# Forming one weight sum of a Strassen-like product by accumulating DMA transfers instead of VectorE adds

## Chip, cores and metric

The kernel runs on one core of a Trainium2 chip. The metric is the device time of one execution in microseconds. TensorE multiplies, VectorE and ScalarE work on tiles, GpSimd is nearly unused here, and SyncE (SP) and ScalarE issue the DMA transfers of the kernel before.

## The reference

One decoder layer on 512 tokens of width 2048: RMSNorm, one wide input projection, three branches (differential attention, dilated attention, gated short convolution), three sigmoid gates, an output projection and a final norm. All in float32. What matters here is the part of the projection that yields branch C's four inputs and the three gates:

```python
proj = jnp.einsum('bsd,df->bsf', h, w_in[l])
...
gates = jax.nn.sigmoid(parts[9 + 3 * n_g] + gate_b[l]).reshape(bsz, seq, N_BRANCH, D_MODEL)
u = jnp.pad(cc * cx, ((0, 0), (C_CONV - 1, 0), (0, 0)))
conv = sum(conv_w[l][j] * u[:, j:j + seq] for j in range(C_CONV))
yc = cb * conv * jax.nn.silu(cz)
merged = (gates[:, :, 0] * jnp.einsum('bsw,wd->bsd', ya, w_branch_a[l]) + ...)
```

## The kernel before, in words

TensorE works in float32r, a reduced form of float32, and recovers the precision by splitting each operand into a high and a low part; every product is three matmuls (lines 519 to 521). ScalarE makes the high half of a weight unit (128 x 1024) into one of three slots w_hi (line 841), VectorE the low half w_lo (line 1227), and TensorE uses the slot for 12 matmuls. A slot can be filled again when TensorE is through with it, so ScalarE and VectorE run up to three units ahead.

The first half of the kernel (to about 1440 us) projects and computes attention for eight heads. Then come ten **quads** (QUADS_G = 10): each multiplies the activations by four weight quarters W11, W12, W21, W22 (2 MB each) with seven products instead of eight, in the manner of Strassen and Winograd. A quad has 28 steps, four units for each of the seven products, and a step takes TensorE about 2.7 us. Quads 0 to 3 give branch C's inputs (stored to c_dram), quads 4 to 9 (from QUADS_C = 4) the gates. The products need four sums of weights, which are formed in place, unit by unit (u = 0 to 3), in three tiles of 2 MB: k2 (loaded with W22), k3 (W21) and k1 (W11):

- R1: k2 = W22 + W21 (line 1245, for the second product)
- R3: k3 = W21 + W11 (line 1248, fifth product)
- R2: k1 = W11 + k2 (line 1251, third product)
- R4: k1 = k1 + W12 (line 1254, sixth product)

In quads 1 to 9 VectorE does these 16 adds per quad between the low halves: R3 in steps 0 to 3, R2 in steps 4 to 7, R4 in steps 12 to 15, and R1 for the next quad in steps 24 to 27. The semaphore sum_done counts them, and summed(kind, q, u) gives the count to wait for. Quad 0 takes sums made earlier.

The order on every engine is written out by hand. SP loads in a fixed order: the W12 units u = 0 to 2 into the ring raw; after the last R2 of the quad the next W22 into k2 (line 459, one 2 MB load); the last W12 unit, when the first R4 has freed its slot; the W22 units into raw; from step 20 the next W21 into k3 (line 471, 2 MB) and four units of W11 into k1 (line 407).

Beside quads 4 to 9 runs **branch C's tail**: eight heads, 20 steps each, from step 8 of quad 4. Per head ScalarE issues four loads of 256 KB in pieces of 512 bytes (rows<-c_dram, line 1029) at its steps 0, 4, 8 and 10. ScalarE reads the first in step 2 (tanh, line 1042), VectorE the second in step 6 (line 1561), and both others in step 12 (line 1564). VectorE also does five more small operations (lines 1557, 1568, 1572 twice, 1575), and TensorE two groups of four transposes (lines 700 and 705). VectorE evicts the products to gin (line 1530), ScalarE makes the gates of them (line 1005) and stores them (line 1015).

Of the kernel before, what the change touches and what calls it, by code (L numbers as in the profile page):

```python
# [33 lines left out]
HU = 8 * P  # L34
# [24 lines left out]
QUADS_C, QUADS_G, QUADS_O = 4, 10, 2  # L59
QUADS_B, STEPS_B, NU = 6, 14, 4  # L60
# [9 lines left out]
W11, W12, W21, W22 = range(4)  # L70
# [15 lines left out]
R1, R3, R2, R4 = range(4)  # L86
# [31 lines left out]
def ring_12(q, u):  # L118
    return X_K + 8 * (q - 1) + u


def ring_22(q, u):
    return ring_12(q, u) + NU


def summed(kind, q, u):
    return 16 * (q - 1) + 4 * kind + u + 1


def weights(p):  # L130
# [31 lines left out]
def program(nc, wst, wg, ws, x_t, x_tok, cols_d, rows_d, lam_d, const_d, out_d):  # L162
    f32, f32r = mybir.dt.float32, mybir.dt.float32r
    ALU, ACT, AX = mybir.AluOpType, mybir.ActivationFunctionType, mybir.AxisListType
# [5 lines left out]
    with ExitStack() as ctx:  # L170
# [3 lines left out]
        def sem(name):  # L174
            return ctx.enter_context(nc.semaphore(name))
# [94 lines left out]
        k2, k3, k1 = [[kb[:, 4096 * n + HU * u:4096 * n + HU * (u + 1)] for u in range(NU)] for n in range(3)]  # L270
# [44 lines left out]
        res_in = [sem(f"res_in{i}") for i in range(4)]  # L315
        raw_in = [sem(f"raw_in{i}") for i in range(RING)]
        k1_in = [sem(f"k1_in{i}") for i in range(NU)]
        k2_in, k3_in = sem("k2_in"), sem("k3_in")
        brow_in, grow_in = sem("brow_in"), sem("grow_in")
        yraw_in, gin_in = sem("yraw_in"), [sem(f"gin_in{i}") for i in range(4)]  # L320
        osum_in, osum_done, osum_stored = sem("osum_in"), sem("osum_done"), sem("osum_stored")
# [20 lines left out]
        sum_done, got, gate_done = sem("sum_done"), sem("got"), sem("gate_done")  # L342
# [9 lines left out]
        block = ctx.enter_context(nc.Block())  # L352
# [473 lines left out]
        def _(act):  # L826
# [12 lines left out]
            def hi_of(r, src):  # L839
                act.wait_ge(pe_used, r + 1)  # L840
                nc.scalar.activation(w_hi[r % RING][:, :], src, ACT.Copy).then_inc(hi_done, 1)  # L841

            def hi_ring(r, x):
                act.wait_ge(raw_in[(W1 + x) % RING], 16 * ((W1 + x) // RING + 1))
                hi_of(r, raw[(W1 + x) % RING][:, :])

            def hi_g(q, n):

                p, u = divmod(n, NU)
                r = R_G + STEPS * q + n  # L850
                if q == 0:
                    hi_ring(r, n)
                elif p == 0:
                    act.wait_ge(k1_in[u], 16 * q)
                    hi_of(r, k1[u])
                elif p == 1:
                    act.wait_ge(sum_done, summed(R1, q, u))
                    hi_of(r, k2[u])
                elif p == 2:
                    act.wait_ge(sum_done, summed(R2, q, u))  # L860
                    hi_of(r, k1[u])
                elif p == 4:
                    act.wait_ge(sum_done, summed(R3, q, u))
                    hi_of(r, k3[u])
                elif p == 5:
                    act.wait_ge(sum_done, summed(R4, q, u))
                    hi_of(r, k1[u])
                else:
                    hi_ring(r, ring_12(q, u) if p == 3 else ring_22(q, u))
# [15 lines left out]
            for k in range(KT):  # L885
                if k in SPLIT_AT:
                    n = SPLIT_AT.index(k)
# [304 lines left out]
            nc.scalar.activation(res[:, 0, 0:3 * C], res[:, 0, 0:3 * C], ACT.Copy, scale=fcol[:, 0:1]).then_inc(fin_s, 1)  # L1192


        @block.vector
        def _(dve):
            steps = {"base": 0, "n": 0, "i": 0, "per": 0}

            def link(ins):

                steps["n"] += 1
                ins.then_inc(dve_step, 1)
                done = steps["base"] + steps["n"]
                dve.wait_ge(dve_step, steps["per"] * steps["i"] + done if steps["per"] else done)
# [24 lines left out]
            def lo_g(q, n):  # L1229

                p, u = divmod(n, NU)
                if q == 0:
                    src = raw[(W1 + n) % RING][:, :]
                else:
                    src = (k1[u], k2[u], k1[u], raw[(W1 + ring_12(q, u)) % RING][:, :], k3[u], k1[u],
                           raw[(W1 + ring_22(q, u)) % RING][:, :])[p]
                lo_of(R_G + STEPS * q + n, src)

            def add_units(kind, q, u):

                if kind == R1:
                    if u == 0:
                        dve.wait_ge(k2_in, 16 * q)
                        dve.wait_ge(k3_in, 16 * q)
                    ins = tt(k2[u], k2[u], k3[u], ALU.add)
                elif kind == R3:
                    dve.wait_ge(k1_in[u], 16 * q)
                    ins = tt(k3[u], k3[u], k1[u], ALU.add)
                elif kind == R2:
                    dve.wait_ge(sum_done, summed(R1, q, u))  # L1250
                    ins = tt(k1[u], k1[u], k2[u], ALU.add)
                else:
                    dve.wait_ge(sum_done, summed(R2, q, u))
                    ins = tt(k1[u], k1[u], raw[(W1 + ring_12(q, u)) % RING][:, :], ALU.add)
                ins.then_inc(sum_done, 1)
# [32 lines left out]
            for k in range(KT):  # L1288
                if k in SPLIT_AT:
                    n = SPLIT_AT.index(k)  # L1290
# [262 lines left out]
            def tail(h, at):  # L1553

                if at == 3:
                    dve.wait_ge(c_th, h + 1)
                    stt(c_z, c_b, 1.0, c_z, ALU.add, ALU.mult).then_inc(c_silu, 1)
                if at == 6:
                    dve.wait_ge(c_silu, h + 1)
                    dve.wait_ge(c_in, 64 * h + 32)  # L1560
                    tt(c_b, c_b, c_z, ALU.mult).then_inc(c_v, 1)
                if at == 12:
                    dve.wait_ge(c_in, 64 * h + 64)
                    tt(c_z, c_z, c_b, ALU.mult).then_inc(c_u, 1)
                taps = [cols[:, S_CONV + 3 * h + n:S_CONV + 3 * h + n + 1] for n in range(3)]
                if at == 15:
                    dve.wait_ge(c_ut, h + 1)
                    link(ts(c_b, u_ps[:, :], taps[2], None, ALU.mult))
                if at == 16:
                    for n in (1, 0):  # L1570
                        d = 2 - n
                        link(stt(c_b[:, d:T], u_ps[:, 0:T - d], taps[n], c_b[:, d:T], ALU.mult, ALU.add))
                if at == 17:
                    dve.wait_ge(c_vt, h + 1)
                    stt(c_b, c_b, 0.5, v_ps[:, :], ALU.mult, ALU.mult).then_inc(c_y, 1)

            for q in range(QUADS_G):
                for n in range(STEPS):
                    if q or n >= RING:
                        lo_g(q, n)  # L1580
                    h, at = divmod(STEPS * q + n - TAIL, TAIL_STEP)
                    if 0 <= h < HEADS:
                        tail(h, at)
                    if q and n == 2:
                        take_g(q - 1, 6)
                    if q and n < 4:
                        add_units(R3, q, n)
                    if q and 4 <= n < 8:
                        add_units(R2, q, n - 4)
                    if q and 12 <= n < 16:  # L1590
                        add_units(R4, q, n - 12)
                    if 24 <= n and q < QUADS_G - 1:
                        add_units(R1, q + 1, n - 24)
                    if q == 0 and n == 3:
                        join_b(HEADS - 1)
                    if q == 0 and n == 4:
                        dve.wait_ge(comb_sum, 2)
                        link(stt(f4, f2, -1.0, as_f32[21][0], ALU.mult, ALU.subtract))
                    if q == 0 and n == 6:
                        comb_low(t2[1], f2, t2[0], 2)  # L1600
                    if q == 0 and n == 8:
                        link(tt(f3, as_f32[22][1], as_f32[12][1], ALU.subtract))
                    if q == 0 and n == 9:
                        link(tt(f3, f3, as_f32[22][0], ALU.add))
                    if q == 0 and n == 11:
                        tt(f3, f3, as_f32[12][0], ALU.subtract).then_inc(comb_sum, 1)
                    if q == 0 and n == 13:
                        comb_low(t3[1], f3, t3[0], 3)
                    if q == 0 and n == 17:
                        tt(f4, f4, as_f32[21][1], ALU.subtract).then_inc(comb_sum, 1)  # L1610
                    if q == 0 and n == 20:
                        comb_low(t4[1], f4, t4[0], 4)
                    if n in EVICT_AT:
                        take_g(q, EVICT_AT[n])
                    if q == QUADS_G - 1:
                        if n in (16, 17, 20, 24):
                            sum_y(0, (P5, P6, P7, P4)[(16, 17, 20, 24).index(n)])
                        if n in (18, 19, 25, 27):
                            low_y(0, (18, 19, 25, 27).index(n))
# [255 lines left out]
```

## Time and profile before

| | us |
|---|---|
| median of 3 runs | 2585.72 |
| lowest and highest | 2584.49 and 2587.26 |
| profiled execution | 2582.52 |
| its span | 2580.7 |

| engine | busy us | share |
|---|---|---|
| TensorE matmuls | 2550.9 | 99% |
| TensorE weight loads | 2102.6 | 81% |
| VectorE | 1836.4 | 71% |
| ScalarE | 986.6 | 38% |
| GpSimd | 0.2 | 0% |

The profile is of one execution, and its times are read as from the start of its span. TensorE's granted clock was full throughout (0.998 of full speed as a mean). Matmuls are pipelined, so a busy TensorE is told by the pitch of its matmuls, and a wait shows at the weight load before the first matmul of a step.

### The profile page before, as it was taken

To read this page: it belongs to the slowest core of one execution; us is meant where nothing else is said; L and a number is where in the kernel's file an instruction comes from. 1 tells how busy PE (TensorE), PEld (TensorE's weight loads), DVE (VectorE), ACT (ScalarE), POOL (GpSimd) and SP (SyncE) were. 2 spreads that over 40 slices of the span, in tenths; PEclk is the share of its full clock that TensorE was granted. 3 is DMA by queue.
4 is the path that set the end of the run, shared out by engine and by line. 5 is a ranking of instruction groups with operands and counts; after the bars stand their busy time and mean duration, and the time that the engine had idled before them with its cause. 6 is when DMAs were issued, how large, how long until landed. Compare 5 with 4: busy or idle time off the path is not lost.

```text
span 2580.7 us, 31181 instructions
## 1 busy us (share of the span) xinstructions
PE 2550.9 (99%) x11758; PEld 2102.6 (81%) x11758; DVE 1836.4 (71%) x2180; ACT 986.6 (38%) x1230; POOL 0.2 (0%) x4
## 2 busy tenths in 40 slices
PE   9999999999999999999999999999999999999998
PEld 7888888888888888888888788888887888788776
DVE  7556656656666566566657877888878888898875
ACT  5332322322323223233333433334444445655644
POOL 0000000000000000000000000000000000000000
PEclk9999999999999999999999999999999999999999
DMA  5235546555455465554223754455565556787565
GB/s 191 87 106 196 196 148 223 182 193 200 148 199 197 146 229 180 193 196 145 88 89 122 269 188 160 140 185 196 192 208 177 161 188 219 269 283 243 202 228 194
DMA packets 147620, 474.72 MB, mean 184 GB/s; under 512 B 12561, under 2 KB 29202, under 8 KB 144786
## 3 DMA queue, kind: packets, MB, share of 16 engines
q1 hardware_dynamic: 89024, 332.15, 37.4%
q10 hardware_dynamic: 58450, 140.59, 15.3%
q8 instruction: 96, 1.57, 0.3%
q14 instruction: 50, 0.41, 0.0%
HBM read 390.90 MB, written 81.79 MB: 183 GB/s over the span
## 4 chain that ended last, share of the span: by engine, by line
PE 88%; DVE 6%; DMA 4%; ACT 1%; issue 1%; SPq 0%; ACTq 0%; DVEq 0%
PE proj L519 18%; PE proj L521 18%; PE proj L520 18%; PE sc_ps L519 4%; PE sc_ps L521 4%; PE sc_ps L520 4%; PE tr_ps L519 4%; PE tr_ps L521 4%; PE tr_ps L520 4%; PE o_ps L521 3%; PE o_ps L520 3%; PE o_ps L519 2%; DVE w_lo L1227 2%; PE tr_ps L560 2%; DMA raw<-s_dram 1%; DMA rows<-c_dram 1%
## 5 line engine op out<-in xcount | busy, mean ns | idle before, releaser
L519 PE MATMUL proj<-act_hi,w_hi 128*128 128x512 f32 x1792 | 709.2, 396 | 2.4 <-DVE w_lo L1223 2.0
L521 PE MATMUL proj<-act_hi,w_lo 128*128 128x512 f32 x1792 | 699.5, 390 | 0.0
L520 PE MATMUL proj<-act_lo,w_hi 128*128 128x512 f32 x1792 | 698.3, 390 | 0.0
L1223 DVE TENSOR_TENSOR w_lo<-raw,w_hi 128x1024 fp32r<-128x1024 f32 x224 | 274.2, 1224 | 265.4 <-ACT w_hi L837 264.6
L837 ACT ACTIVATE w_hi<-raw 128x1024 fp32r<-128x1024 f32 x224 | 236.6, 1057 | 519.0 <-PE proj L521 513.2
L519 PEld LDWEIGHTS proj<-act_hi,w_hi 128*128 128x128 f32 x1792 | 336.8, 188 | 71.2 <-DVE w_lo L1223 2.1
L521 PEld LDWEIGHTS proj<-act_hi,w_lo 128*128 128x128 f32 x1792 | 336.4, 188 | 71.5
L520 PEld LDWEIGHTS proj<-act_lo,w_hi 128*128 128x128 f32 x1792 | 337.0, 188 | 66.6
L1227 DVE TENSOR_TENSOR w_lo<-raw,w_hi 128x1024 fp32r<-128x1024 f32 x240 | 293.0, 1223 | 131.1 <-ACT w_hi L841 130.4
L841 ACT ACTIVATE w_hi<-raw 128x1024 fp32r<-128x1024 f32 x240 | 254.5, 1060 | 336.8 <-PE proj L521 89.0
L841 ACT ACTIVATE w_hi<-kb 128x1024 fp32r<-128x1024 f32 x180 | 190.9, 1061 | 269.0 <-PE sc_ps L521 91.0
L1227 DVE TENSOR_TENSOR w_lo<-kb,w_hi 128x1024 fp32r<-128x1024 f32 x180 | 219.6, 1222 | 73.1 <-ACT w_hi L841 72.9
L906 ACT ACTIVATE sc<-sc,nmax 128x768 f32<-128x768 f32 (+4 forms) x96 | 65.5, 683 | 194.7 <-DVE nmax L1367 103.0
L519 PE MATMUL tr_ps<-w_hi,tb 128*128 128x512 f32 x264 | 103.7, 393 | 0.8 <-DVE w_lo L1227 0.8
L521 PE MATMUL tr_ps<-w_hi,tb 128*128 128x512 f32 x264 | 102.8, 390 | 0.0
L520 PE MATMUL tr_ps<-w_lo,tb 128*128 128x512 f32 x264 | 102.8, 390 | 0.0
L519 PE MATMUL sc_ps<-w_hi,act_hi 128*128 128x512 f32 x248 | 97.4, 393 | 3.2 <-DVE w_lo L1227 3.2
L520 PE MATMUL sc_ps<-w_lo,act_hi 128*128 128x512 f32 x248 | 96.6, 390 | 0.0
L519 PE MATMUL tr_ps<-w_hi,act_hi 128*128 128x512 f32 x232 | 91.3, 394 | 1.6 <-DVE w_lo L1227 1.6
L520 PE MATMUL tr_ps<-w_lo,act_hi 128*128 128x512 f32 x232 | 90.4, 390 | 0.0
L920 ACT ACTIVATE qk_hi<-stage 128x512 fp32r<-128x512 f32 x32 | 20.2, 632 | 182.0 <-DVE stage L1353 140.9
L519 PE MATMUL sc_ps<-w_hi,tb 128*128 128x512 f32 x224 | 87.8, 392 | 1.1 <-DVE w_lo L1227 0.6
(309 smaller groups left out, 3976.8 us busy)
## 6 DMA issues: line engine op xcount, KB each, us to landing
raw<-wst SPq DMA_DIRECT2D x224, 512.0 KB, 3.5
ssum<-ws ACTq DMA_DIRECT2D x24, 2048.0 KB, 9.2
s_dram<-ssum ACTq DMA_DIRECT2D x24, 2048.0 KB, 7.5
raw<-s_dram SPq DMA_DIRECT2D x96, 512.0 KB, 4.3
raw<-ws SPq DMA_DIRECT2D x72, 512.0 KB, 4.2
kb<-wg SPq DMA_DIRECT2D x18, 2048.0 KB, 8.5
raw<-wg SPq DMA_DIRECT2D x72, 512.0 KB, 3.9
kb<-wg SPq DMA_DIRECT2D x36, 512.0 KB, 7.1
```

The costliest lines, as they stand in the source:

```text
L519: nc.tensor.matmul(out, w_h, a_h, start=first, stop=False, skip_group_check=shared)
L520: nc.tensor.matmul(out, w_h, a_l, start=False, stop=False, skip_group_check=shared)
L521: return nc.tensor.matmul(out, w_l, a_h, start=False, stop=last, skip_group_check=shared)
L560: end = nc.tensor.transpose(tr_ps[idx % 2][:, n * P:(n + 1) * P], tile, ident[:, :])
L837: nc.scalar.activation(w_hi[slot_w][:, :], raw[slot_raw][:, :], ACT.Copy).then_inc(hi_done, 1)
L841: nc.scalar.activation(w_hi[r % RING][:, :], src, ACT.Copy).then_inc(hi_done, 1)
L906: end = nc.scalar.activation(tile[:, lo:hi], tile[:, lo:hi], ACT.Exp, scale=scale, bias=nmax[:, m:m + 1], accum_out=sums[:, m:m + 1])
L920: nc.scalar.activation(qk_hi[w][:, :], blk[w][:, :], ACT.Copy).then_inc(qh_done, 1)
L1223: tt(w_lo[slot_w][:, :], raw[slot_raw][:, :], w_hi[slot_w][:, :].bitcast(f32), ALU.subtract).then_inc(lo_done, 1)
L1227: tt(w_lo[r % RING][:, :], src, w_hi[r % RING][:, :].bitcast(f32), ALU.subtract).then_inc(lo_done, 1)
```

## The change

For quads 4 to 9 the sum R1 is no longer formed by VectorE. SP loads W22 into k2 as before and W21 into k3 as before; as soon as the load of k2 has landed, GpSimd issues four DMA transfers of 512 KB that read W21 from DRAM once more and add it to k2 in place. A semaphore for each unit, r1_done, tells when it has landed. ScalarE (high halves of k2, second product) and VectorE (R2) wait for r1_done in place of sum_done; VectorE's R3 now waits for the load of k3 itself, which R1 did for it. VectorE forms the other three sums, 12 adds per quad, and summed counts accordingly. The R1 of quads 1 to 3 stays with VectorE.

```diff
 def summed(kind, q, u):
-    return 16 * (q - 1) + 4 * kind + u + 1
+    if q < QUADS_C:
+        return 16 * (q - 1) + 4 * kind + u + 1
+    return 16 * (QUADS_C - 1) + 12 * (q - QUADS_C) + 4 * (kind - R3) + u + 1
@@ ScalarE, hi_g
                 elif p == 1:
-                    act.wait_ge(sum_done, summed(R1, q, u))
+                    if q < QUADS_C:
+                        act.wait_ge(sum_done, summed(R1, q, u))
+                    else:
+                        act.wait_ge(r1_done[u], 16 * (q - QUADS_C + 1))
                     hi_of(r, k2[u])
@@
+        @block.gpsimd
+        def _(pool):
+
+            for q in range(QUADS_C, QUADS_G):
+                pool.wait_ge(k2_in, 16 * q)
+                for u in range(NU):
+                    pool.dma_start(k2[u], wg[q, W21, :, HU * u:HU * (u + 1)], accum_op=ALU.add).then_inc(r1_done[u], 16)
@@ VectorE, add_units
                 elif kind == R3:
+                    dve.wait_ge(k3_in, 16 * q)
                     dve.wait_ge(k1_in[u], 16 * q)
                     ins = tt(k3[u], k3[u], k1[u], ALU.add)
                 elif kind == R2:
-                    dve.wait_ge(sum_done, summed(R1, q, u))
+                    if q < QUADS_C:
+                        dve.wait_ge(sum_done, summed(R1, q, u))
+                    else:
+                        dve.wait_ge(r1_done[u], 16 * (q - QUADS_C + 1))
                     ins = tt(k1[u], k1[u], k2[u], ALU.add)
@@ VectorE, quads
-                    if 24 <= n and q < QUADS_G - 1:
+                    if 24 <= n and q < QUADS_C - 1:
                         add_units(R1, q + 1, n - 24)
```

## Rows read from the trace of the kernel before

**Rows 1.** The page, busy time of each engine.
```profile
PE 2550.9 (99%) x11758; PEld 2102.6 (81%) x11758; DVE 1836.4 (71%) x2180; ACT 986.6 (38%) x1230; POOL 0.2 (0%) x4
```

**Rows 2.** Busy time by stretch: length, PE, PEld, DVE, ACT, POOL, clock, DMA share.
```profile
1640.50:1716.70 76.20, 76.20 (x338) 63.14 (x337) 60.97 (x60) 29.72 (x28) 0.00 (x0) 1.00 0.50 173
1874.70:1956.20 81.50, 79.46 (x348) 64.06 (x347) 67.51 (x70) 35.50 (x39) 0.00 (x0) 1.00 0.55 184
```

**Rows 3.** Waits of TensorE's weight loads, 1716 to 2116: total us, times, longest.
```profile
PEld sc_ps L519 <- DVE w_lo L1227: 4.3, 4, 1.6
PEld tr_ps L519 <- DVE w_lo L1227: 3.5, 5, 1.2
```

**Rows 4.** The same, 1920 to 1950; then two waits outside, in the timeline.
```profile
PEld tr_ps L519 <- DVE w_lo L1227: 2.9, 4, 1.2
PEld sc_ps L519 <- DVE w_lo L1227: 1.4, 2, 0.8
...
1840.52 0.19 PEld L519 LDWEIGHTS sc_ps<-w_hi,act_hi 128*128 128x128 f32 x1 [1.61 <-DVE w_lo L1227]
...
2078.46 0.19 PEld L519 LDWEIGHTS sc_ps<-w_hi,act_hi 128*128 128x128 f32 x1 [1.36 <-DVE w_lo L1227]
```

**Rows 5.** Chain that ended last, behind the cluster's last wait: start, us, what.
```profile
1944.10 0.50 PE tr_ps L519
```

**Rows 6.** SP's load of W21 (timeline), and the late branch C load (chain).
```profile
2063.02 0.33 SPq L471 DMA_DIRECT2D kb<-wg  x1
...
2063.63 11.54 DMA rows<-c_dram
```

**Rows 7.** Timeline of ScalarE and VectorE where they waited for these loads.
```profile
1837.62 0.63 ACT L1042 ACTIVATE rows<-rows 128x512 f32<-128x512 f32 x1 [5.30 <-DMA rows<-c_dram]
...
1921.86 0.69 DVE L1564 TENSOR_TENSOR rows<-rows 128x512 f32<-128x512 f32 x1 [3.73 <-DMA rows<-c_dram]
...
2075.26 0.69 DVE L1561 TENSOR_TENSOR rows<-rows 128x512 f32<-128x512 f32 x1 [4.11 <-DMA rows<-c_dram]
```

**Rows 8.** Group of VectorE's R1 adds, 1716 to 2116: busy us, mean ns, idle.
```profile
L1245 DVE TENSOR_TENSOR kb<-kb 128x1024 f32<-128x1024 f32 x20 | 24.4, 1220 | 0.1
```

**Rows 9.** DMA issues by kind: size and median us from issue to landing.
```profile
s_dram<-ssum ACTq DMA_DIRECT2D x24, 2048.0 KB, 7.5
...
kb<-wg SPq DMA_DIRECT2D x18, 2048.0 KB, 8.5
raw<-wg SPq DMA_DIRECT2D x72, 512.0 KB, 3.9
...
rows<-c_dram ACTq DMA_DIRECT2D x32, 256.0 KB, 3.8
```

**Rows 10.** Timeline: W22 load into k2, its reader; branch C loads and readers.
```profile
1716.70 0.33 SPq L459 DMA_DIRECT2D kb<-wg  x1
...
1781.33 1.06 ACT L841 ACTIVATE w_hi<-kb 128x1024 fp32r<-128x1024 f32 x1 [1.66 <-PE proj L521]
...
1726.19 0.38 ACTq L1029 DMA_DIRECT2D rows<-c_dram  x1
...
1733.63 0.69 DVE L1561 TENSOR_TENSOR rows<-rows 128x512 f32<-128x512 f32 x1
...
1884.39 0.38 ACTq L1029 DMA_DIRECT2D rows<-c_dram  x1
...
1889.10 0.61 ACT L1042 ACTIVATE rows<-rows 128x512 f32<-128x512 f32 x1
...
1969.48 0.37 ACTq L1029 DMA_DIRECT2D rows<-c_dram  x1
...
1977.55 0.69 DVE L1564 TENSOR_TENSOR rows<-rows 128x512 f32<-128x512 f32 x1
```

**Rows 11.** Timeline of quad 3: SP issues the last W12 unit, ScalarE reads it.
```profile
1653.28 9.36 SPq L390 DMA_DIRECT2D raw<-wg  x4
...
1657.95 1.06 ACT L841 ACTIVATE w_hi<-raw 128x1024 fp32r<-128x1024 f32 x1 [1.66 <-PE proj L521]
```

More of the change, by code:

```diff
@@ L317, in program @@
         k1_in = [sem(f"k1_in{i}") for i in range(NU)]
-        k2_in, k3_in = sem("k2_in"), sem("k3_in")
+        k2_in, k3_in, r1_done = sem("k2_in"), sem("k3_in"), [sem(f"r1_done{i}") for i in range(NU)]
         brow_in, grow_in = sem("brow_in"), sem("grow_in")
```

## The prediction

> **What bounds the kernel now.** I read the page's busy table first: TensorE is busy for 2550.9 of 2580.7 us [rows 1], so at most some 30 us can be won in the whole kernel. Then the table by stretch: quad 3, which has no branch C work beside it, takes 76.2 us, and the quad from 1874.7 takes 81.5 us [rows 2]. VectorE is busy for 61 us of the one and 67.5 of the other, so it isn't the bound on average; what counts is where TensorE waits.
>
> TensorE's own waits from 1716 to 2116 us, the quads that the change touches, come to 4.3 + 3.5 = 7.8 us in nine waits, all for VectorE's low halves (line 1227) [rows 3]. Six of the nine stand in one cluster between 1920 and 1950, 1.4 + 2.9 = 4.3 us; two of the others are of 1.61 and 1.36 us [rows 4]. Each wait costs a little more than its own length: in the chain that ended last the first matmul behind one takes 0.50 us [rows 5], against 76.2 / 336 = 0.23 us in quad 3 [rows 2]. I take 0.23 more per wait, a little less than the difference, so the cluster is worth 4.3 + 6 x 0.23 = 5.7 us and all nine 7.8 + 9 x 0.23 = 9.9 us.
>
> What is behind the waits is in the chain: a small load of branch C (rows<-c_dram, 256 KB) took 11.5 us [rows 6], three times in all with a spread of 0.3 us, against a median of 3.8 us [rows 9]. It was issued 0.6 us behind SP's 2 MB load of W21 [rows 6], on which four 512 KB loads of W11 follow, 4 MB together; the other two met the same traffic. ScalarE waited 5.30 us for the first, VectorE 3.73 and 4.11 us for the others [rows 7]. These loads are late because of DMA traffic, not of VectorE. VectorE enters behind the middle one: after it, the four adds that the change removes (line 1245) stand between the late low halves, and the cluster is their backlog.
>
> **Part 1, four adds fewer on VectorE.** Per quad from 4 on, four adds of 1.22 us go; 20 of them lie in the window, 24.4 us [rows 8], 24 in the kernel, 29 us. Nearly all of it lies under TensorE. Behind the middle late load VectorE worked nearly without a pause from 1921.86 to TensorE's last wait at 1944.10 [rows 5, 7], and the four adds are 4 x 1.22 = 4.9 us of that. The largest single wait of the cluster is 1.2 us [rows 4], and the low halves come 1.2 us earlier after the first add, 4.9 after the fourth. So I take the whole cluster as gone: -5.7 us. The 5.30 us wait is on ScalarE, and the 4.11 us wait is followed by evictions and low halves, without such an add; those two waits of TensorE stay. The ninth, 7.8 - 4.3 - 1.61 - 1.36 = 0.5 us, may go or stay. The bounds of this part are 0 and -9.9 us.
>
> **Part 2, the new waits.** ScalarE (second product) and VectorE (adds R2) now wait for r1_done. Accumulation for quad 5 can begin when W22 has landed, 8.5 us [rows 9] after 1716.70 [rows 10], near 1725; the first reader is ScalarE's high half of k2 at 1781.33 [rows 10]. That is 56 us for four transfers. The wait is passed without a stop even if they take four times as long as four loads. R3 now waits for the W21 load, as R1 did, two steps and more later; 0 us. GpSimd is idle today (0.2 us busy [rows 1]), and nothing is queued on it behind its wait. Shorter counting of sum_done changes no order on SP: 0 us.
>
> **Part 3, four accumulating transfers per quad, 2 MB.** No row shows an accumulation. Its bounds: as a load of the same 2 MB, 8.5 us; or as that load plus the reading of 2 MB from the on-chip memory, for which the nearest row is the 2 MB store, 7.5 us, together 16 us [rows 9]. What hides them is that nobody waits for them; what they cost is what they slow. They begin about 1.5 us after W22 has landed (estimate: as nothing of GpSimd's issue is in the trace, 0 to 3), and these branch C loads then meet them, with their readers [rows 10]:
> - quad 4: issued 1726.19, read by VectorE (line 1561) at 1733.63: 7.4 us allowed.
> - quad 6: issued 1884.39, read by ScalarE (line 1042) at 1889.10: 4.7 us allowed.
> - quad 7: issued 1969.48, read by VectorE (line 1564) at 1977.55: 8.1 us allowed.
>
> Quads 5 and 8 have their loads before or late behind the accumulation, quad 9 has no accumulation; nothing there.
>
> How long does such a load take beside 2 MB of accumulation? At least 11.5 us, if it behaves as beside the 4 MB of SP [rows 6]; at most 11.5 + 7.5 = 19 us, with the second reading on top. I take 14, a third of the way, since 11.5 is the row of the same load beside traffic that is as large, if an accumulation is counted as reading twice. The waits are then 14 - 7.4 = 6.6, 14 - 4.7 = 9.3 and 14 - 8.1 = 5.9 us. Not all reaches TensorE: VectorE's wait of 4.11 us [rows 7] gave 1.36 + 0.23 = 1.6 us [rows 4] (2.5 us swallowed), ScalarE's of 5.30 us gave 1.61 + 0.23 = 1.8 (3.5 swallowed). So 4.1 + 5.8 + 3.4 = **+13.3 us**. At 11.5 us it is 1.6 + 3.3 + 0.9 = +5.8 us, at 19 us 9.1 + 10.8 + 8.4 = +28.3 us; and 0 if a small load isn't held up at all.
>
> The last W12 load of each quad also meets them. In quad 3 it is issued at 1653.28 and used at 1657.95, 4.7 us later [rows 11], and ScalarE has those 3.5 us of slack: 8.2 us allowed. Such loads take 3.9 us as a median [rows 9]. Doubled it is 7.8, still within: 0 us; trebled, as the small load was beside SP's, 11.7, and in the three quads without another wait 3 x 3.5 = 10.5 us, kept for the upper end.
>
> **Sum.** -5.7 + 13.3 = +7.6 us. The profiled execution took 2582.5 us (span 2580.7), 3.2 below the median of the runs; 2582.5 + 7.6 = 2590.1, and against the median 2585.7 + 7.6 = 2593.3 us.
>
> A rule that bears on the upper bound: "Collectives: The Full Stack" of the Trainium skill (The bandwidth ceiling: the fold count and why AG ≠ RS ≠ AR) says that a reduction in the DMA engines is limited by its two source reads, not by the addition, and comes out at about half the rate of a copy. No run here shows it yet; by it the accumulation would be at the 16 us end, and the double-reading rival below would hold.
>
> **Rivals.**
> - *The transfers hide, and the cluster goes.* If an engine serves a branch C load ahead of accumulations, or these are thin enough in time, part 3 is 0 to 2 us and the result -5.7 to -3.7: about 2581. For it: the DMA engines are busy for only 0.50 to 0.55 of the two quads shown [rows 2]. Against it: the same small load trebled its time each time it met SP's large ones.
> - *Break-even.* The small loads take 11.5 us as beside SP's traffic: +5.8 - 5.7 = 0, 2585.8 us.
> - *Double reading, the slow side.* An accumulation reads source and destination through the same 16 engines; each branch C load that meets it takes 19 us: +28.3 - 5.7 = +22.6, 2608 us; more if the last W12 load passes 8.2 us too (+10.5). It decides from the point where such a load takes more than 11.5 us: there the loss passes the gain of 5.7. For it: there is nothing else in the change that TensorE could wait for. Against it: no row.
> - *The change does what it says and nothing follows*, since the late loads and not VectorE make the waits: both parts near 0. It lies within the break-even case.
>
> **Chances.** Forecast case (+2 to +15 us): 0.35. Hidden (-9 to -2): 0.25. Break-even (-2 to +2): 0.15. Double reading (+15 and more): 0.25. A measurement of this kernel can tell about 0.2%, 5.2 us, from no change. Slower by more: the double case and some 0.22 of the forecast case, 0.47. Faster by more: the lower half of the hidden case and a little, 0.19. Within: 0.34. The range leaves out the top of the double case (beyond +25 us) and the bottom of the hidden one: 2578 to 2611 us. The likeliest case alone is 2588 to 2601 us.
>
> **What would show it.** VectorE's adds at line 1245 fall from 36 to 12 and its busy time by 29 us. Right: the cluster behind the late branch C load of quad 6 is gone; the loads of 1726, 1884 and 1969 take 11.5 to 19 us, with waits at lines 1561, 1042 and 1564 and TensorE's waits right behind them. Wrong: those loads land in 4 to 6 us (then the kernel is faster by about 5 us), the W12 load is waited for in each quad, or anyone waits for r1_done. Wrong in another way: the accumulation is still running when SP loads W21 at step 20 of the quad, 30 us later; then it prolongs the late loads that exist today too, and the kernel is slower than my range.

## The result, and the profile after

The changed kernel takes 2594.35 us (median of 20 executions, 2587.45 to 2604.66) against 2584.43 us (20 executions, 2581.04 to 2588.62) for the kernel before on the same chip: ratio 1.0041, 95% interval 1.0032 to 1.0049. It is slower by 9.9 us. The forecast was 2593.3 us. The profiled execution has a span of 2590.4 us, 9.7 more than before, at a granted clock of 0.997 against 0.998 on average. A part of the loss is a stretch at half clock, shown below.

The page, first the busy time of each engine and then GpSimd's DMA queue (packets, MB, share of the time of 16 DMA engines):

```profile
PE 2553.0 (99%) x11758; PEld 2103.6 (81%) x11758; DVE 1810.7 (70%) x2156; ACT 985.6 (38%) x1230; POOL 21.6 (1%) x28
...
q0 software_dynamic: 3456, 12.58, 2.6%
```

VectorE has 24 instructions and 26 us less than in [rows 1], as the change says; GpSimd has 24 transfers. 2.6% of 2590 us, divided by 24, is 2.8 us on all 16 engines for one accumulation of 512 KB.

The DMA issues by kind (count, size, median us from issue to landing), to be held against [rows 9]:

```profile
kb<-wg SPq DMA_DIRECT2D x18, 2048.0 KB, 8.3
raw<-wg SPq DMA_DIRECT2D x72, 512.0 KB, 4.8
kb<-wg POOLq DMA_DIRECT2D x24, 512.0 KB, 9.9
rows<-c_dram ACTq DMA_DIRECT2D x32, 256.0 KB, 4.0
```

Now who waits, 1716 to 2125 us (engine, line and what for: total us, times, longest). In the kernel before the first of these lines was 7.7 us in 3 waits of at most 3.6:

```profile
ACT w_hi L843 <- DMA raw<-wg: 32.7, 7, 6.2
...
PEld sc_ps L521 <- DVE w_lo L1240: 9.1, 5, 4.1
ACT rows L1047 <- DMA rows<-c_dram: 8.0, 2, 7.8
DVE rows L1581 <- DMA rows<-c_dram: 6.1, 2, 3.6
DVE rows L1578 <- DMA rows<-c_dram: 4.7, 2, 4.5
PEld tr_ps L521 <- DVE w_lo L1240: 4.3, 5, 1.8
...
PEld o_ps L521 <- DVE w_lo L1240: 1.1, 2, 0.6
```

ScalarE now waits for the W12 loads. What happens is seen in full in quad 3, where no branch C work runs: the timeline (start, us, engine, line, what; in brackets the idle time before it and what ended it).

```profile
1648.88 2.80 POOL L1206 DMA_DIRECT2D kb<-wg  x3 [1648.43 <-DMA kb<-wg]
1654.69 0.89 POOL L1206 DMA_DIRECT2D kb<-wg  x1 [3.01 <-issue]
...
1662.33 1.06 ACT L843 ACTIVATE w_hi<-raw 128x1024 fp32r<-128x1024 f32 x1 [5.90 <-DMA raw<-wg]
...
1664.70 0.19 PEld L521 LDWEIGHTS o_ps<-w_hi,act_hi 128*128 128x128 f32 x1 [1.69 <-DVE w_lo L1240]
1664.81 0.19 PEld L522 LDWEIGHTS o_ps<-w_lo,act_hi 128*128 128x128 f32 x1
1665.04 0.19 PEld L523 LDWEIGHTS o_ps<-w_hi,act_lo 128*128 128x128 f32 x1
```

and the same stretch by windows (length, busy PE, PEld, DVE, ACT, POOL, clock, DMA share, GB/s):

```profile
1649.00:1653.00 4.00, 4.00 (x19) 3.34 (x18) 2.50 (x3) 1.41 (x2) 2.68 (x3) 1.00 0.62 96
1653.00:1657.00 4.00, 4.00 (x20) 3.30 (x19) 3.28 (x4) 1.77 (x2) 0.89 (x1) 1.00 1.04 196
1657.00:1661.00 4.00, 4.00 (x19) 3.31 (x18) 3.15 (x4) 0.00 (x0) 0.00 (x0) 1.00 1.04 265
1661.00:1665.00 4.00, 2.73 (x12) 1.99 (x11) 1.58 (x2) 2.67 (x3) 0.00 (x0) 1.00 1.03 306
```

GpSimd starts the accumulations 4.5 us ahead of SP's issue of the last W12 load, and from 1653 to 1665 the DMA engines are fully busy. The kernel before had 0.02 from 1649 to 1653 and 0.44 to 0.70 behind it. The load is read 8.9 us after its issue instead of 4.7 [rows 11]; ScalarE's slack is used up, and TensorE waits 1.69 us. In quads 3 to 8 the loads were read 8.92, 8.77, 8.39, 7.80, 9.70 and 7.40 us after issue (before: 4.67, 4.69, 4.08, 4.68, 5.16, 3.72), and each time TensorE waited.

TensorE's waits sum to 16.19 us in 13 (the three PEld rows of the table above and the 1.69 us of quad 3), against 7.82 in nine [rows 3]. What a wait costs is read from the pitch of the weight loads: behind the wait of 1.69 us the second load comes 0.11 us after the first and the next 0.23 later, the usual pitch, so TensorE is 1.5 us late. Each wait costs about 0.15 us less than its length, not 0.23 more, as the prediction has it.

One wait costs more. Behind the one of 4.13 us TensorE's granted clock is at its lower level, 1.2 GHz (0.50), and the loads come every 0.43 us instead of 0.23 until 1852.5:

```profile
1847.21 0.29 PEld L521 LDWEIGHTS sc_ps<-w_hi,act_hi 128*128 128x128 f32 x1 [4.13 <-DVE w_lo L1240]
...
1847.81 0.33 PEld L523 LDWEIGHTS sc_ps<-w_hi,act_lo 128*128 128x128 f32 x1
1848.24 0.33 PEld L521 LDWEIGHTS sc_ps<-w_hi,act_hi 128*128 128x128 f32 x1
```
```profile
1846.00:1852.00 6.00, 4.78 (x11) 3.79 (x12) 4.12 (x4) 2.95 (x4) 0.00 (x0) 0.50 0.63 180
1853.00:1859.00 6.00, 6.00 (x28) 4.96 (x27) 4.28 (x5) 2.65 (x3) 0.00 (x0) 1.00 0.70 247
```

By cause, as delays of TensorE: behind the six W12 loads eight waits of 9.0 us, +7.8; the late branch C load of quad 5 became later, +2.8, and the half clock behind it +2.3; quad 7's branch C load and its followers, +0.6; the cluster of [rows 4] is gone, -3.3; small rest, +0.2. That is 10.4 us. From SP's issue of the last W12 load in quad 1 to the same in quad 9 the kernel takes 633.64 us instead of 623.16, 10.5 more.

The branch C loads: how the one of quad 6 was issued and read, the readers' waits in quads 6 and 7, and three rows of the chain that ended last (start, us, what):

```profile
1892.04 2.66 POOL L1206 DMA_DIRECT2D kb<-wg  x3 [79.25 <-DMA kb<-wg]
...
1892.41 0.38 ACTq L1034 DMA_DIRECT2D rows<-c_dram  x1
1898.28 0.62 ACT L1047 ACTIVATE rows<-rows 128x512 f32<-128x512 f32 x1
...
1989.86 0.69 DVE L1581 TENSOR_TENSOR rows<-rows 128x512 f32<-128x512 f32 x1 [2.47 <-DMA rows<-c_dram]
```
```profile
1827.44 3.71 DMA y_dram<-rows
1831.17 13.14 DMA rows<-c_dram
...
1975.57 14.27 DMA rows<-c_dram
```

Of the three loads that were to meet the accumulations, those of quads 4 and 6 were issued 0.9 and 0.4 us behind GpSimd's first (1727.89 against 1727.02, 1892.41 against 1892.04), ahead of the bulk of the traffic. They landed after 5.8 us each, and their readers didn't wait. The one of quad 7 took 14.27 us, about as forecast, and its reader waited 2.47 us. The 4.13 us belong to quad 5's load, which was late before too (1.61 us [rows 4]).

### The profile page after: what moved, and what is told of

Its sections match the earlier page's. It is cut to its first block, busy times and chain, and to the rows that moved or that the text cites. A ratio compares the mean times of both kernels' runs of the same rounds, so it can differ in the third digit from the quotient of the medians.

```text
span 2590.4 us, 31211 instructions
## 1 busy us (share of the span) xinstructions
PE 2553.0 (99%) x11758; PEld 2103.6 (81%) x11758; DVE 1810.7 (70%) x2156; ACT 985.6 (38%) x1230; POOL 21.6 (1%) x28
## 4 chain that ended last, share of the span: by engine, by line
PE 87%; DMA 6%; DVE 4%; ACT 1%; issue 1%; SPq 0%; DVEq 0%; ACTq 0%
PE proj L521 17%; PE proj L523 17%; PE proj L522 17%; PE sc_ps L521 4%; PE sc_ps L523 4%; PE sc_ps L522 4%; PE tr_ps L521 4%; PE tr_ps L523 4%; PE tr_ps L522 4%; PE o_ps L523 2%; PE o_ps L521 2%; PE o_ps L522 2%; PE tr_ps L562 2%; DVE w_lo L1240 2%; DMA raw<-wg 2%; DMA rows<-c_dram 2%
## 5 line engine op out<-in xcount | busy, mean ns | idle before, releaser
L523 PE MATMUL sc_ps<-w_hi,act_lo 128*128 128x512 f32 x224 | 88.2, 394 | 0.0
```

The source lines that it names most:

```text
L523: return nc.tensor.matmul(out, w_l, a_h, start=False, stop=last, skip_group_check=shared)
```

## The experiments

All ratios are to the kernel before, run beside them on the same chip. They come in order of what they separate.

**Each part alone.** The first kernel takes only the four adds away: neither VectorE nor a transfer forms W22 + W21, and the readers wait for the load (the sum is left out).

```diff
-        @block.gpsimd ... four accumulations
-                        act.wait_ge(r1_done[u], 16 * (q - QUADS_C + 1))
+                        act.wait_ge(k2_in, 16 * q)
```

> The first part of the change alone: VectorE's 24 R1 adds of quads 4 to 9 are left out and nothing forms that sum (k2 stays W22, so the gates of these quads are computed from wrong weights); no accumulating transfers; the waits are on the load of k2 instead of r1_done. Theory (the adds are worth the cluster of waits behind the late branch C load of quad 6): 4 to 6 us faster than the kernel before, ratio 0.998, the two waits of 1.4 and 1.6 us stay. Rival (the waits come from the late loads alone and the adds under them cost nothing): within 1 us of before.

Measured 2580.04 us, 0.9982 (0.9973 to 0.9991), 4.9 us faster. TensorE's waits in its timeline, all that are left:

```profile
1841.77 0.19 PEld L521 LDWEIGHTS sc_ps<-w_hi,act_hi 128*128 128x128 f32 x1 [2.08 <-DVE w_lo L1232]
2075.52 0.19 PEld L521 LDWEIGHTS sc_ps<-w_hi,act_hi 128*128 128x128 f32 x1 [0.86 <-DVE w_lo L1232]
2108.87 0.19 PEld L521 LDWEIGHTS tr_ps<-w_hi,tb 128*128 128x128 f32 x1 [0.31 <-DVE w_lo L1232]
```

The cluster is gone and the other waits stand, as part 1 of the prediction has it.

The second keeps VectorE's adds and has the accumulations beside them (so W21 is added twice).

```diff
                 if kind == R1:
+                    if q >= QUADS_C:
+                        dve.wait_ge(r1_done[u], 16 * (q - QUADS_C + 1))
                     ins = tt(k2[u], k2[u], k3[u], ALU.add)
```

> The second part alone: VectorE keeps all its R1 adds as in the kernel before, and GpSimd issues the 24 accumulating transfers as well, each R1 add waiting for its transfer (k2 gets W21 twice, so it is a timing run). Theory (the transfers' traffic delays the last W12 load of each of quads 3 to 8 and branch C's loads): 12 to 17 us slower than before, +0.5 to 0.65%, since the gain of the adds is missing. Rival (the transfers are nearly free, and the changed kernel loses time by what the missing adds or the new waits rearrange): within 4 us of before.

Measured 2599.48 us, 1.0054 (1.0039 to 1.0068), +14.6 us. The two parts add up: -4.9 + 14.6 = +9.7 us, the whole change within the intervals.

**Plain loads in place of the accumulations** (the addition is left out; same bytes, queue and moments).

```diff
-  pool.dma_start(k2[u], wg[q, W21, :, HU * u:HU * (u + 1)], accum_op=ALU.add)...
+  pool.dma_start(k2[u], wg[q, W21, :, HU * u:HU * (u + 1)])...
```

> The changed kernel with the 24 transfers as plain loads instead of accumulations (k2 is overwritten with W21; the addition is left out); same bytes from DRAM, same queue, same place. Theory A (traffic of any kind delays the last W12 load): that load still takes over 6 us and the kernel is 3 to 8 us slower than before. Theory B (it is the second reading that costs: the engines' time per transfer falls from 2.8 to 1.5 us): the last W12 load takes 5 to 6 us, TensorE no longer waits for it, and the kernel is within 4 us of before or up to 5 us faster. Rival (GpSimd's queue or its descriptors are the cost): as slow as the changed kernel, +9 to 10 us.

Measured 2581.02 us, 0.9985 (0.9976 to 0.9994). Its page's row of GpSimd's queue and its issue row:

```profile
q0 software_dynamic: 3456, 12.58, 1.4%
...
kb<-wg POOLq DMA_DIRECT2D x24, 512.0 KB, 6.0
```

The same bytes cost half the engine time (1.5 us for 512 KB instead of 2.8) and land in 6.0 us instead of 9.9. Four W12 loads of six are read 5.3 to 6.5 us after issue, and TensorE waits for one only: quad 7's, which took 10.65 us, more than any behind accumulations, and left a wait of 2.94 us. Plain traffic can do the same harm, then; here it did it once in six quads. The median is 1 us above that of the kernel without transfers: a second reading of W21 in itself costs nearly nothing; accumulating it costs some 14 us (1.0041 against 0.9985).

**Is it engine time alone?** Each accumulation is replaced by two plain transfers: one into k2, one from the same weights to DRAM that nobody reads. W21 is loaded over W22, so the sum is left out.

```diff
+  pool.dma_start(k2[u], wg[q, W21, :, ...]).then_inc(r1_done[u], 16)
+  pool.dma_start(junk[q - QUADS_C, u, :, :], wg[q, W21, :, ...]).then_inc(r1_done[u], 16)
```

> The changed kernel with each accumulation replaced by two plain transfers of 512 KB from GpSimd: W21 onto k2 (as in the run with plain loads; the addition is left out) and once more to a DRAM buffer that nobody reads. Theory (an accumulation costs by the engines' time, 2.8 us against 1.5 us of a plain transfer): two plain ones take the same 3 us, the last W12 load takes 8 to 9 us again, and the kernel is 5 to 12 us slower than before. Rival (it is something of the accumulation itself): near the run with plain loads, 2 to 4 us faster than before.

Measured 2583.1 us, 0.9999 (0.999 to 1.0008): neither of the two forecasts, and nearer the rival. In its rows the engine time is that of the accumulations, and the engines are just as full behind the issue of the W12 load:

```profile
q0 software_dynamic: 6912, 25.17, 2.6%
...
1657.00:1661.00 4.00, 4.00 (x19) 3.33 (x18) 3.22 (x4) 0.20 (x1) 0.00 (x0) 1.00 1.01 410
1661.00:1665.00 4.00, 4.00 (x20) 3.29 (x19) 3.11 (x3) 2.87 (x3) 0.00 (x0) 1.00 1.03 423
```

TensorE is at 4.00 of 4.00 in both. By the ratios, about 4 us of the price follow from engine time as such (0.9999 against the 0.9982 of no transfers), and about 11 us appear only when the transfers accumulate (1.0041 against 0.9999).

Where these 11 us lie is told only in part. The W12 loads were read 7.0 to 8.1 us after issue, the changed kernel's 7.4 to 9.7. In quads 3 to 7 about one microsecond makes the difference: behind the plain transfers TensorE waits at most 0.35 us at a time (in quad 3, load read after 7.3 us, not at all), behind the accumulations up to 1.99 (in quad 3, 8.9 us, 1.69). In quad 8 it waits as long behind the eight plain transfers (1.71 us, load read after 7.3) as behind the four accumulations (1.81 us, 7.4). Together the W12 loads make 5 to 6 us of the difference between the two profiled executions. Most of the rest is quad 5's branch C load, with the half clock behind it, and there the order of two issues decides: here the load was issued at 1826.42 us, 0.8 us ahead of SP's 2 MB load, and landed after 2.9 us; in the changed kernel it was issued 0.15 us behind it (1831.17 against 1831.02) and took 13.14. The kernel with both parts, which is slow too, also had it ahead (by 0.36 us, 3.2 us to land). So this order isn't shown to be an effect of accumulating.

**Fewer accumulations.** Two of the four, the other two sums left out:

```diff
-                for u in range(NU):
+                for u in range(2):
```

> The changed kernel with two of the four accumulations per quad; the sum of the other two units is left out (they stay W22). Theory with a threshold (TensorE waits only when the last W12 load takes over 8 us or so): that load takes 6 to 7.5 us, TensorE's waits for it all but vanish, and the kernel is 1 to 5 us faster than before. Rival (cost in proportion to the number of transfers, half of 14.6 us): 2 to 3 us slower than before.

Measured 2581.97 us, 0.9988 (0.9979 to 0.9997). Half of the transfers cost 1.6 us (0.9988 against 0.9982 without any, intervals of 2.3 us either way), all of them 14.6 us: the price isn't proportional. That fits a threshold; but the two that are left out are also the ones that are issued closest to the W12 load, and the runs don't tell number and nearness apart. The W12 loads took 6.4, 6.2, 5.2, 7.3, 8.6 and 3.4 us.

In one quad only (quad 7's sum, which takes the adds behind the middle late load off VectorE; all other sums by VectorE):

```diff
-            for q in range(QUADS_C, QUADS_G):
+            pool.wait_ge(k2_in, 16 * ONE)      # ONE = 7
+            for u in range(NU):
+                pool.dma_start(k2[u], wg[ONE, W21, ...], accum_op=ALU.add)...
```

> The kernel before, with the accumulating transfers in one place only: the R1 of quad 7, whose four VectorE adds stand in the backlog behind the late branch C load of quad 6. All sums are formed; VectorE adds R1 in every other quad. Theory (the whole gain of the missing adds comes from this one place, while each quad's accumulations cost their own 1 to 3 us at the W12 load): the cluster is gone, about 1 us of new waits at quad 6's W12 load, 3 to 4.5 us faster than before, ratio 0.9985. Rival (the gain is spread over the quads, a sixth here): within 1 us of before.

Measured 2584.23 us, 1.0001 (0.9992 to 1.001): a miss for the theory. The cluster is gone (two waits of 0.16 and 0.27 us come at 2012 and 2015, in quad 7), but quad 6's W12 load took 8.34 us (chain), and TensorE waited 1.13 and 0.28 us behind it. The wait at 1842 us was 2.72 us instead of 1.61. It stands ahead of the first accumulation (1886.66), where this kernel does what the kernel before does, so it shows how much a single wait differs between executions. A gain of 3 us in one place is hard to tell from that.

```profile
1890.15 8.34 DMA raw<-wg
...
1900.88 0.19 PEld L524 LDWEIGHTS o_ps<-w_hi,act_hi 128*128 128x128 f32 x1 [1.13 <-DVE w_lo L1241]
```

**Other moments for the same work.** If the W12 loads are the price, it should go when the accumulations start behind them:

```diff
                 pool.wait_ge(k2_in, 16 * q)
+                x = W1 + ring_12(q - 1, 3)
+                pool.wait_ge(raw_in[x % RING], 16 * (x // RING + 1))
```

> The changed kernel with one wait more on GpSimd: the four accumulations of a quad start only when the last W12 load of the quad before has landed, some 5 us later than in the changed kernel. All sums are formed. Theory (the last W12 load is the main loss, 9 us of waits in quads 3 to 8): that load is back at 4 us, ScalarE's waits for it are gone, and the kernel is 0 to 6 us faster than before, depending on branch C's loads in quads 4, 6 and 7, which still meet the transfers. Rival (branch C's small loads are the main loss, as in the prediction): still 6 us or more slower than before.

Measured 2601.36 us, 1.0056 (1.0042 to 1.0071): slower than the changed kernel by 4 us (by the ratios) to 7 us (by the medians), though the intervals of the two touch. The theory, 0 to 6 us faster, missed. The W12 waits did go (loads read 3.6 to 5.2 us after issue), and now branch C's loads meet the accumulations. Rows of its chain, and TensorE behind the last of them:

```profile
1744.73 16.56 DMA rows<-c_dram
...
1903.10 13.45 DMA rows<-c_dram
...
2063.59 16.38 DMA rows<-c_dram
```
```profile
2079.99 0.63 ACT L1047 ACTIVATE rows<-rows 128x512 f32<-128x512 f32 x1 [9.93 <-DMA rows<-c_dram]
...
2082.88 0.29 PEld L521 LDWEIGHTS o_ps<-w_hi,act_hi 128*128 128x128 f32 x1 [6.24 <-DVE w_lo L1242]
```

This is the forecast's branch C mechanism at its forecast size (14 us, 11.5 to 19), at other places than it was forecast for. Later still, behind step 16 of the quad:

```diff
+                pool.wait_ge(lo_done, R_G + STEPS * (q - 1) + 16)
```

> The changed kernel with the accumulations started at step 16 of the quad (GpSimd waits for the low half of step 15), behind the last W12 load and some 11 us later than in the changed kernel. All sums are formed. Theory (an accumulation trebles or quadruples the time of whatever small load meets it, so what counts is which load that is): no wait for W12, but branch C's loads of steps 16 to 24 in quads 4, 6 and 8 take 13 to 17 us and the end of the accumulations meets SP's load of W21 at step 20; slower than before by 8 to 18 us. Rival (past the W12 load there is slack everywhere): 3 to 5 us faster than before.

Measured 2605.96 us, 1.0077 (1.0064 to 1.009), 20 us slower and a little above the theory's 18; the W12 waits are gone, and the chain has branch C loads of 17.73, 15.11 and 16.78 us. One at a time, behind steps 15, 17, 25 and 27:

```diff
+                    pool.wait_ge(lo_done, R_G + STEPS * (q - 1) + (16, 18, 26, 28)[u])
```

> The changed kernel with the four accumulations of a quad spread: the first may start behind step 15, the others behind steps 17, 25 and 27. All sums are formed. Theory (a small load is held up by as many accumulations as are queued at once, so one at a time costs it 3 us and not 10): no load takes over 10 us beside them, TensorE's waits are as without the adds, and the kernel is 0 to 5 us faster than before. Rival (an accumulation costs by its engine time wherever it is put): 5 us or more slower than before.

Measured 2590.2 us, 1.0019 (1.0011 to 1.0028). An accumulation now lands in 7.9 us and the transfers' price is down by a third (1.0019 instead of 1.0041, above the same 0.9982), but both forecasts missed (0 to 5 us faster; 5 us or more slower). Small loads above 10 us are five in its trace. Four of them (11.5 to 12.8 us) are those that SP's traffic makes late in the kernel before too (11.4 to 12.7). The fifth was issued at 2083.76 us, 0.6 us behind an accumulation, and took 10.6 us instead of 6.3; VectorE waits 2.87 us for it and TensorE five times behind that, 3.4 us in all. Of the four places tried for the start, none is free of a reader that is nearly late.

**The changed kernel again**, unchanged, beside these:

> The changed kernel unaltered, on the same chip as the others of this group, to compare them with. Every theory: 9 to 11 us slower than before.

Measured 2595.21 us, 1.0039 (1.0026 to 1.0053). Its trace shows which of the causes hold from one execution to the next. The W12 loads do: eight waits of 8.3 us, against 9.0. The branch C loads don't: quad 5's costs 1.80 us instead of 4.13, quad 7's took 16.16 us, and quads 7 and 8 have waits that the first trace lacks, with half clock behind them:

```profile
1846.70 0.19 PEld L521 LDWEIGHTS sc_ps<-w_hi,act_hi 128*128 128x128 f32 x1 [1.80 <-DVE w_lo L1240]
...
1990.37 0.42 PEld L707 LDWEIGHTS proj<-ident,rows 128*128 128x128 f32 x4 [2.52 <-DVE rows L1581]
...
2090.25 0.71 PEld L702 LDWEIGHTS proj<-ident,rows 128*128 128x128 f32 x4 [2.70 <-DVE rows L1578]
```

**GpSimd adds by itself** instead of by transfers (no DMA traffic is added):

```diff
-  pool.dma_start(k2[u], wg[q, W21, ...], accum_op=ALU.add).then_inc(r1_done[u], 16)
+  nc.gpsimd.tensor_tensor(k2[u], k2[u], k3[u], ALU.add).then_inc(r1_done[u], 1)
```

> The changed kernel with GpSimd adding k3 to k2 itself, four adds of 128 x 1024 per quad, instead of issuing transfers; VectorE's R3 waits for them, since they read k3. All sums are formed, and no DMA traffic is added. Theory (only the extra traffic makes the change slow): if GpSimd's adds take under 3 us each and don't stretch VectorE's, 3 to 5 us faster than before. Rival (the two engines share a way to the on-chip memory, or R3 waits for GpSimd at the start of the quad): VectorE's adds and low halves get longer than 1.22 us where they meet GpSimd's, or R3 starts late, and the kernel is 2 us or more slower than before.

Measured 2592.51 us, 1.0032 (1.0021 to 1.0042). The groups of its page (count | busy us, mean ns | idle) and a row of its timeline:

```profile
L1206 POOL TENSOR_TENSOR kb<-kb 128x1024 f32<-128x1024 f32 x24 | 70.4, 2966 | 2017.9 <-DMA kb<-wg 2017.9
...
1687.28 9.84 DVE L1240 TENSOR_TENSOR w_lo<-raw,w_hi 128x1024 fp32r<-128x1024 f32 x3 [0.18 <-ACT w_hi L843]
```

Each add takes 2.97 us on GpSimd beside VectorE's work, and while it runs VectorE's low halves take 3.3 us instead of 1.22. VectorE's busy time is 1841.0 us against 1810.7 in the changed kernel and 1836.4 before [rows 1]: all that was taken off it comes back on it. The rival's forecast holds.

**Half and half, everything computed.** Accumulations for units 0 and 1, VectorE adds units 2 and 3 in steps 26 and 27 as in the kernel before:

```diff
-                for u in range(NU):
+                for u in range(2):
@@
-                    if 24 <= n and q < QUADS_C - 1:
+                    if (24 if q < QUADS_C - 1 else 26) <= n and q < QUADS_G - 1:
```

> Each quad forms two of its four sums by accumulation (column groups 0 and 1) and the other two by VectorE, in the steps where the kernel before has them; everything is computed. Theory, a threshold (TensorE begins to wait when the W12 load takes more than about 7.5 us, which the run with two accumulations stayed under in five quads of six): W12 loads 5 to 7.5 us, TensorE's waits as in the run with half of the accumulations, and half of the adds' cost is given back: 1 to 4 us faster than before (0.9985 to 0.9997). Rival, the cost of an accumulation is proportional to its number (13.6 us for 24, so 6.8 us for 12, against half of 4.9 us of adds): 2 to 5 us slower than before (1.0008 to 1.002).

Measured 2583.86 us, 0.9996 (0.9987 to 1.0005). The proportional price (1.0008 and more) is ruled out by the interval; the gain, if there is one, is below what can be told. Its timeline shows why it is so small: the cluster, which two adds in place of four should thin out, is down to three waits of six, and TensorE now waits behind quad 6's W12 load (0.78 and 0.28 us) and quad 7's (0.77).

```profile
1899.95 0.19 PEld L521 LDWEIGHTS o_ps<-w_hi,act_hi 128*128 128x128 f32 x1 [0.78 <-DVE w_lo L1240]
...
1939.55 0.19 PEld L521 LDWEIGHTS tr_ps<-w_hi,act_hi 128*128 128x128 f32 x1 [0.52 <-DVE w_lo L1240]
1942.42 0.19 PEld L521 LDWEIGHTS tr_ps<-w_hi,act_hi 128*128 128x128 f32 x1 [0.24 <-DVE w_lo L1240]
1946.01 0.19 PEld L521 LDWEIGHTS tr_ps<-w_hi,act_hi 128*128 128x128 f32 x1 [1.00 <-DVE w_lo L1240]
```

No version that forms all the sums was measurably faster than the kernel before.

## Why the prediction was right, and where only its sum was

**What bounds the kernel** held. All of the loss that the trace locates stands at TensorE's waits and at the half clock behind the longest, and the new waits go back to loads that came late through traffic. The price of a wait was misread: the matmul behind it takes 0.50 us [rows 5], but the next weight load starts 0.11 us after the first, so a wait costs 0.15 us less than its length and not 0.23 more.

**Part 1** held: -5.7 forecast, -4.9 us measured with the adds alone, with the cluster gone and the other waits in place. With the right price per wait the cluster is worth 3.3 us in the trace; the interval of the measurement (2.3 to 7.0 us) takes in both.

**Part 2** held: no engine waits for r1_done in the trace after. The last accumulation of quad 3 is issued at 1654.69 and lands near 1667; the k2 units are read from about 1705 on (1781.33 [rows 10], one quad of 76.2 us earlier).

**Part 3** had the right kind of cost and the right total, +14.6 us measured alone against +13.3, but the wrong terms:

- *The branch C loads of quads 4, 6 and 7, +13.3 us forecast.* Of these only quad 7's was struck: +0.6 us in the first trace and +3.0 in the second. What was added elsewhere on branch C's loads had been forecast at nothing: in the first trace 2.8 us in quad 5 and 2.3 at half clock, in the second 2.9 us in quad 8 and some 3 at half clock. The failing step is the moment: the accumulations' start was put near 1726.5, and a load issued at 1726.19 was counted as fully behind the traffic. But GpSimd needs 5.8 us from its first issue to its last, and the engines fill up only 4 us after the first (0.62 from 1649 to 1653), so a load issued within a microsecond of the start slips through and lands 5.8 us later. Two of the three loads thus landed "in 4 to 6 us", which was to be the sign of a faster kernel; it was slower all the same. What such a load costs when it is really behind the accumulations was sized rightly (14.27 and 16.16 us in quad 7; 13.45 to 17.73 in the two kernels that put the accumulations later); what its reader allows was not (8.1 us forecast, 14.27 - 2.47 = 11.8 found).
- *The last W12 load, 0 us forecast, +7.8 us in the trace.* This is the term that was mis-sized. The prediction doubled the load to 7.8 us and allowed 8.2. The load took 7.4 to 9.7, and the wait of 1.69 us behind 8.92 puts the allowance at 7.2 us (7.1 to 7.9 in the first three quads). It was worked out from quad 3 alone: in quad 8 ScalarE waits for this load in the kernel before too (read 3.7 us after issue), and there the allowance is only 7.40 - 1.81 = 5.6 us. A term that stands 0.4 us below its threshold and recurs six times should have been carried with a price and not at zero. The prediction had it, as "trebled", at 10.5 us in the upper end, and "the W12 load is waited for in each quad" as a sign of error: that sign came.
- *An accumulation's own time.* Forecast 8.5 to 16 us for 2 MB. In quad 3 the first is issued at 1648.88 and the last lands near 1667, so 2 MB take some 18 us, 6 of them GpSimd's issuing.

The sum, +7.6 forecast and +9.9 us measured, is therefore right by luck, through errors of opposite sign: in the first trace 13.3 - 0.6 = 13 us of loss too many at the three branch C loads, against 7.8 us missing at the W12 loads, 5.1 at quad 5's load with the half clock, and a gain at the cluster taken 2.4 us too large.

That the transfers "hide" is ruled out by the second kernel; "double reading" had the property of the chip right (2.8 against 1.5 us of engine time) and the price wrong, since it multiplied the time of three loads of which two mostly missed the traffic. That the second half of the engine time is the reading of the destination fits the numbers; no run shows it directly.

"Collectives: The Full Stack" of the Trainium skill (The bandwidth ceiling: the fold count and why AG ≠ RS ≠ AR) says of the reduction in a collective that it runs at about half the rate of a copy, because of its two source reads. The engine time of the accumulating transfer here agrees (1.9 times). The kernel with two plain transfers for each accumulation shows that this alone doesn't give the price: it is about 11 us faster.

## What to carry to other kernels

The accumulating DMA took about twice the engine time of the same copy here, and the kernel lost more by it than by two copies in its place: before moving an add into one, list every load issued from its start to its landing, the loads of the neighbouring stage too, with the slack of its reader in each repetition, and carry a term that is within a microsecond of its threshold at a price, times the number of its repetitions. Take a second trace of the same kernel before a single wait is put down to a cause. An add that is free under TensorE (here all but 5 of 29 us) has little to give, and a transfer issued in its place costs from the point where one reader's slack is gone.

## What the runs showed of the hardware

- An accumulation of 512 KB takes 2.8 us of all 16 DMA engines and lands in 9.9 us (median of rows of four), a plain load of the same from the same queue 1.5 and 6.0 us.
- GpSimd's record of issuing an accumulation lasts 0.9 to 1.6 us (quad 3, median 1.1; three begin within 1.2 us and end 2.8 us after the first began), that of a plain load 0.53 us. The fourth accumulation of a quad was issued 3.0 to 4.4 us after the third had been, and of eight plain transfers in a row the eighth was held up by 2.3 to 2.9 us; what holds it isn't in the profile.
- A float32 add of 128 x 1024 takes 2.97 us on GpSimd beside VectorE's work, against 1.22 on VectorE alone, and VectorE's own two-input operations are stretched to 3.3 us beside it.
- A TensorE wait of 4.13 us was followed by half the granted clock until 1852.5 us; the loads' pitch was 0.43 us instead of 0.23 there, which cost 2.3 us more. Behind the waits of up to 1.99 us in the same trace the pitch was the usual one.
- A branch C load of 256 KB issued 0.36 or 0.8 us ahead of SP's 2 MB load landed after 3.2 and 2.9 us; issued 0.15 us ahead of it or behind it, after 11.1 to 13.1.
- Open: why a W12 load is read 8.9 us after issue behind four accumulations and 7.3 us behind eight plain transfers of the same engine time. The eight are issued a little later (to 1655.9 us), and their issue was not aligned with that of the four, so the order of the queues and something in the accumulation itself are not told apart.
- Executions of the changed kernel spread over 17 us and those of the kernel before over 8 in the same comparison. Waits near a threshold would do that, and so would two issues whose order changes; it wasn't tested.
